# Prompt attention: probabilities scaled in place by GpSimd and turned by plain transposes, in place of fp32 products with diagonals of factors

## The chip, the core and the metric

The kernel runs on one core of a Trainium2 chip. The metric is the device time of one execution in microseconds, the median over repeated runs. The engines are TensorE (PE in the profile), VectorE (DVE), ScalarE (ACT), GpSimd (POOL) and SyncE (SP), each with its own queue, in order, tied together by semaphores.

## What is computed

One inference step of a hybrid decoder layer for 1024 prompt rows and 32 sample rows: half-step FFN, a mixer (attention with three branches and a pooling mixer), a second half-step FFN, and a final norm. The change is in the mixer's attention for the prompt. It has 8 query heads of 64 in two groups, each group with one key/value head. For each head and query row there are three softmaxes: over the compressed keys (64 blocks), over the selected keys (at 16 blocks of 64, all 1024 causal keys), and over a window of 512. Their outputs are added, each with a gate:

```
def masked_softmax(s, mask):
    s = jnp.where(mask, s, NEG_INF)
    m = jnp.max(s, axis=-1, keepdims=True)
    e = jnp.where(mask, jnp.exp(s - m), 0.0)
    return e / jnp.maximum(jnp.sum(e, axis=-1, keepdims=True), 1e-30)

o = gates[..., 0:1] * o_c + gates[..., 1:2] * o_s + gates[..., 2:3] * o_w
```

## The kernel before

The kernel is a row of stages; behind each, all engines meet at a barrier. The order: sample compression, first FFN, input projection, pooling, prompt compression, prompt attention (`stage_attend_prompt`, the only stage that the change touches), sample attention, output projection, second FFN, final norm.

Prompt attention loops over the 2 groups of heads and, in each, over 9 steps. Step `qt` (0 to 7) makes the scores of query tile `qt` (128 query rows) for its four heads, one head at a time: the selected scores over (`qt` + 1) x 128 keys into `slc_bank`, the window and compressed scores into `win_bank`. VectorE finds the maxima (L1744, L1748, L1750). ScalarE writes the exponentials into `probs[qt % 2]` and their sums into `sums` (L1648, L1654, L1656). After the second and the fourth head VectorE works out the factors, gate over sum, for that pair of heads (`factors`, L1704 to L1712).

The same step turns the probabilities of the query tile before, so that keys stand in the partitions, and multiplies them with the values. The work of a tile is cut into units by `value_units`: a unit is one tile of keys of one branch for all four heads. Query tile 0 to 7 has 3, 5, 7, 9, 11, 12, 13 and 14 units, the selected ones first, then the window's, then the compressed one; both groups together have 148. A quarter of a tile's units goes behind each head's scores. The ninth step has no scores, only the 14 units of query tile 7.

A unit goes through four engines' hands. TensorE turns it into one of two banks (`turn`, L1775). ScalarE copies the bank rounded to `turned_hi` (L1624), VectorE writes what was rounded off to `turned_lo` (L1689), and TensorE adds two products with the values into `out_bank` (`value_product`, L1839, L1840). TensorE issues the turn of a unit before the products of the unit ahead of it (`pending`). The banks also serve to turn keys and queries: GpSimd writes each query tile twice over into `dup` (L1582) and TensorE turns it by transposes (L1781). ScalarE's order in a head is: the copy of the first turn, the selected exponential, the copy of the second, the other two exponentials, the rest. VectorE's is: the maxima, then the remainders, then the factors.

The turn of a unit also applies the factors. GpSimd writes, for each pair of heads, six diagonal matrices of the factors (`diagonals`, L1591: the identity times the factors), and `turn` is an fp32 product of the probabilities with such a diagonal, one for each of the four heads. The first unit of a tile waits until both pairs' diagonals are there.

Of the kernel before, what the change touches and what calls it, by code (L numbers as in the profile page):

```python
# [24 lines left out]
ALU = mybir.AluOpType  # L25
AX = mybir.AxisListType

P = 128
# [11 lines left out]
HD, N_HEADS, N_KV, GROUP = 64, 8, 2, 4  # L40
# [1430 lines left out]
def stage_attend_prompt(nc, mem, K, z, kcp, vcp, mixT):  # L1471
# [12 lines left out]
    QT = SEQ // P  # L1484
    WT = WINDOW // P
    NB = SEQ // CMP_STRIDE
    WIN0, CMP0 = SEQ, SEQ + (WT + 1) * P
    PW = CMP0 + NB
    CMP, SLC, WIN = 0, 1, 2
    HEADS = QT * GROUP  # L1490
    PAIR = 2

    def win_tiles(qt):
        return list(range(max(0, qt - WT + 1), qt + 1)) + ([qt - WT] if qt >= WT else [])

    def value_units(qt):
        return ([(SLC, t * P, P, (0, t)) for t in range(qt + 1)]
                + [(WIN, WIN0 + i * P, P, (1, t)) for i, t in enumerate(win_tiles(qt))]
                + [(CMP, CMP0, NB, None)])
# [21 lines left out]
    at = {x: n for n, x in enumerate(order)}  # L1521
    dups = {x: n for n, x in enumerate([x for x in order if x[0] != "v"])}
    products = {x: n for n, x in enumerate([x for x in order if x[0] == "v"])}
    TURNS, DUPS, PRODUCTS = len(order), len(dups), len(products)
    assert TURNS % 2 == 0 and DUPS % 2 == 0 and PRODUCTS % 2 == 0

    ONE, RING = 1, 2
    PE_ORDER, ACT_ORDER, DVE_ORDER = (0, 0), (1, 2), (0, 0)

    with ExitStack() as scope:  # L1530
# [7 lines left out]
        kT_hi = mem.sb(scope, "at_kT_hi", [P, 2, SEQ], F32R)  # L1538
        kT_lo = mem.sb(scope, "at_kT_lo", [P, 2, SEQ], F32R)
        probs = [mem.sb(scope, f"at_probs{i}", [P, GROUP, PW]) for i in range(2)]  # L1540
        diag = mem.sb(scope, "at_diag", [P, 2, GROUP, 3, P])
        neg_max = mem.sb(scope, "at_neg_max", [P, 2, GROUP, 3])
        sums = mem.sb(scope, "at_sums", [P, 2, GROUP, 3])
        factor = mem.sb(scope, "at_factor", [P, 2, GROUP, 3])
# [9 lines left out]
        dup_ready, turned, hi_done, split = (mem.sem("at_dup_ready"), mem.sem("at_turned"),  # L1554
                                             mem.sem("at_hi_done"), mem.sem("at_split"))
# [1 line left out]
        scored = [mem.sem(f"at_scored{i}") for i in range(2)]  # L1557
        maxed = [mem.sem(f"at_maxed{i}") for i in range(2)]
        exped = [mem.sem(f"at_exped{i}") for i in range(2)]
        factor_ready, diag_ready = mem.sem("at_factor_ready"), mem.sem("at_diag_ready")  # L1560
        out_done, upper_done, out_taken = mem.sem("at_out_done"), mem.sem("at_upper_done"), mem.sem("at_out_taken")
        dve_step = mem.sem("at_dve_step")
        STEPS = 2 * 2 * QT + 2
# [1 line left out]
        with nc.Block() as block:  # L1565
            @block.gpsimd
            def _(pool):
                pool.sem_inc(diag_ready, ONE)

                def duplicate(g, x):  # L1570

                    m = dups[x]
                    before = TURNS * g + ONE
                    if m >= 2:
                        before += at[[y for y in dups if dups[y] == m - 2][0]] + 1
                    pool.wait_ge(turned, before)
                    if x[0] == "k":
                        off = (OFF_SLC, OFF_WIN)[x[1]]
                        rows = z[:, 4 * x[2]:4 * x[2] + 4, bass.ds(off + g * HD, HD)]
                    else:  # L1580
                        rows = z[:, x[1], bass.ds(g * GROUP * HD, GROUP * HD)].rearrange("p (r d) -> p r d", r=GROUP)
                    pool.tensor_copy(dup[m % 2][:], rows.unsqueeze(2).to_broadcast([P, 4, 2, HD])).then_inc(dup_ready, 1)  # L1582

                def diagonals(g, qt, pair):
                    pool.wait_ge(factor_ready, 2 * QT * g + 2 * qt + pair + 1)
                    if qt >= 2:
                        last = ("v", qt - 2, len(value_units(qt - 2)) - 1)
                        pool.wait_ge(turned, TURNS * g + at[last] + 1 + ONE)
                    heads = slice(PAIR * pair, PAIR * pair + PAIR)
                    f = factor[:, qt % 2, heads, :]  # L1590
                    pool.tensor_tensor(diag[:, qt % 2, heads].rearrange("p r b n -> p (r b) n"),  # L1591
                                       K["ident"][:].unsqueeze(1).to_broadcast([P, 3 * PAIR, P]),
                                       f.rearrange("p r b -> p (r b)").unsqueeze(2).to_broadcast([P, 3 * PAIR, P]),
                                       ALU.mult).then_inc(diag_ready, 1)

                with pool.Fori(0, N_KV) as g:
                    for x in LEAD:
                        duplicate(g, x)
                    for qt in range(QT):
                        if qt + 1 < QT:  # L1600
                            duplicate(g, ("q", qt + 1))
                        for pair in range(2):
                            diagonals(g, qt, pair)

            @block.scalar
            def _(act):
# [57 lines left out]
            def _(dve):  # L1664
# [28 lines left out]
                def factors(g, qt, pair):  # L1693

                    for i in range(2):
                        dve.wait_ge(exped[i], HEADS * g + GROUP * qt + PAIR * (pair + 1) + ONE)
                    if qt >= 2:
                        dve.wait_ge(diag_ready, 2 * QT * g + 2 * (qt - 2) + pair + 1 + ONE)
                    else:
                        dve.wait_ge(diag_ready, 2 * QT * g + ONE)  # L1700
                    heads = slice(PAIR * pair, PAIR * pair + PAIR)
                    f = factor[:, qt % 2, heads, :]
                    s0 = STEPS * g + (4 * qt + 2 * pair + 2 if qt else 3 * pair)
                    dve.tensor_scalar(f, sums[:, qt % 2, heads, :], 1e-30, None, ALU.max).then_inc(dve_step, 1)  # L1704
                    dve.wait_ge(dve_step, s0 + 1)
                    dve.reciprocal(f, f).then_inc(dve_step, 1)
                    dve.wait_ge(dve_step, s0 + 2)
                    if qt == 0:
                        dve.tensor_scalar(f[:, :, CMP:CMP + 1], f[:, :, CMP:CMP + 1], K["has_block"][:], None,
                                          ALU.mult).then_inc(dve_step, 1)  # L1710
                        dve.wait_ge(dve_step, s0 + 3)
                    dve.tensor_tensor(f, f, z[:, qt, bass.ds(OFF_GATE + g * 3 * GROUP + 3 * PAIR * pair, 3 * PAIR)]  # L1712
                                      .rearrange("p (r b) -> p r b", b=3), ALU.mult).then_inc(factor_ready, 1)
# [12 lines left out]
                with dve.Fori(0, N_KV) as g:  # L1726
# [8 lines left out]
                    for qt in range(QT + 1):  # L1735
                        for r in range(GROUP):
                            if r == 1 and qt >= 2:
                                take(g, qt - 2)
                            n = GROUP * qt + r
# [19 lines left out]
            def _(pe):  # L1759
# [4 lines left out]
                def turn(g, x):  # L1764
                    n = TURNS * g + at[x]
                    bank = turn_bank[at[x] % 2]
                    pe.wait_ge(split, n - 1 + RING)
                    if x[0] == "v":
                        _, qt, u = x
                        branch, lo, rows, _ = value_units(qt)[u]  # L1770
                        if u == 0:
                            pe.wait_ge(diag_ready, 2 * QT * g + 2 * (qt + 1) + ONE)
                        pe.nop(nofuse=True)
                        for h in range(GROUP):
                            tr = pe.matmul(bank[0:rows, h * P:(h + 1) * P], probs[qt % 2][:, h, lo:lo + rows],  # L1775
                                           diag[:, qt % 2, h, branch, :], start=True, stop=True)
                    else:
                        pe.wait_ge(dup_ready, DUPS * g + dups[x] + 1)
                        pe.nop(nofuse=True)
                        for i in range(4):  # L1780
                            tr = pe.transpose(bank[:, i * P:(i + 1) * P],  # L1781
                                              dup[dups[x] % 2][:, i].rearrange("p c d -> p (c d)"), K["ident"][:])
                    tr.then_inc(turned, 1)
# [694 lines left out]
def trunk_step(nc, x_prompt, x_sample, cache_cmp, cache_slc, page_table, state_win, state_pool,  # L2478
# [17 lines left out]
    with ExitStack() as whole:  # L2496
# [21 lines left out]
        with ExitStack() as mixer:  # L2518
            z_sample = mem.sb(mixer, "z_sample", [N_SAMPLE, OFF_POOL])
            with ExitStack() as scope_z:  # L2520
# [22 lines left out]
                with ExitStack() as scope:  # L2543
                    for name, width in (("ident16", P), ("diagonal", P), ("edge", P), ("blocks", 120)):
                        K[name] = mem.sb(scope, name, [P, width], BF16)
                    K["has_block"] = mem.sb(scope, "has_block", [P, 1])
                    with ExitStack() as wide_scope:
                        wide = {name: mem.sb(wide_scope, name + "_wide", [P, width])
                                for name, width in (("diagonal", P), ("edge", P), ("blocks", 120))}
                        stage_constants(nc, mem, [(wide["diagonal"][:], c_diagonal), (wide["edge"][:], c_edge),  # L2550
                                                  (wide["blocks"][:], c_blocks), (K["has_block"][:], c_has_block)],
                                        [(K["ident"][:], K["ident16"][:])]
                                        + [(wide[name][:], K[name][:]) for name in wide])
                    stage_attend_prompt(nc, mem, K, z, kcp[:, 0], vcp[:, 0, 0], trunk)
                    mem.end_stage()
# [87 lines left out]
```

## Time and profile before

| what | value |
|---|---|
| median of 3 runs | 3343.32 us (3338.0 to 3347.6) |
| the profiled execution | 3338.51 us, span 3336.9 us |
| TensorE busy | 2922.3 us, 88% of the span |
| VectorE busy | 1342.8 us, 40% |
| ScalarE busy | 933.8 us, 28% |
| GpSimd busy | 326.9 us, 10% |
| mean granted TensorE clock | 0.929 |

### The profile page before, as it was taken

The numbers are of one execution on the slowest core, as the hardware profiler recorded it, in microseconds if no ns is written. First come the engines' busy times: TensorE is split into PE (matmuls) and PEld (weight loads), VectorE is DVE, ScalarE is ACT, GpSimd is POOL, SyncE is SP. The second block draws the span as 40 slices with busy tenths as digits, with TensorE's granted clock in tenths as the row PEclk, the third lists the DMA queues.
The fourth block names the chain that finished last, engine by engine and source line by source line (L and its number), as shares of the span: only waits on it lengthen the run. The fifth ranks groups of instructions, "written<-read, shape, count | busy, mean of one in ns | idle before, by whom it ended". The sixth has DMA issues, their size and how long they took to land. (4 is left out here: it accounts for less than half of the span.)

```text
span 3336.9 us, 48603 instructions
## 1 busy us (share of the span) xinstructions
PE 2922.3 (88%) x18382; PEld 2686.5 (81%) x18382; DVE 1342.8 (40%) x2566; ACT 933.8 (28%) x1520; POOL 326.9 (10%) x298
## 2 busy tenths in 40 slices
PE   3898878999999997787678789687688999999997
PEld 3898867999999996786567667533587999999996
DVE  6344445433344335113145455322326434344334
ACT  3655633111111112111245445333213111111112
POOL 3444421000000000000011011211001000000000
PEclk9999988999999998898579879888898999999999
DMA  4222132111211102011200000264321111211101
GB/s 155 76 86 108 55 109 91 38 50 38 63 38 38 50 13 86 22 35 42 68 1 1 2 1 1 107 192 152 118 70 38 39 50 38 62 38 38 50 13 52
DMA packets 168573, 193.81 MB, mean 58 GB/s; under 512 B 11432, under 2 KB 154537, under 8 KB 165680
## 3 DMA queue, kind: packets, MB, share of 16 engines
q1 hardware_dynamic: 161623, 141.58, 13.9%
q0 software_dynamic: 6816, 50.49, 4.1%
q8 instruction: 80, 1.31, 0.2%
q14 instruction: 54, 0.43, 0.0%
HBM read 178.30 MB, written 17.91 MB: 59 GB/s over the span
## 5 line engine op out<-in xcount | busy, mean ns | idle before, releaser
L328 ACT ACTIVATE f_act_gate<-f_gate 128x352 f32<-128x352 f32 x132 | 61.2, 465 | 1141.3 <-PE f_gate L104 1141.2
L394 DVE SCALAR_TENSOR_TENSOR trunk<-f_down,trunk 128x352 f32<-128x352 f32 x528 | 276.3, 525 | 209.5 <-PE f_down L104 209.5
L102 PE MATMUL f_gate<-f_h_hi,f_gu_hi 128*128 128x352 f32 x1056 | 343.4, 325 | 15.5 <-DVE f_act_up L370 15.5
L370 DVE TENSOR_TENSOR f_act_up<-f_act_gate,f_up 128x352 f32<-128x352 f32 x132 | 68.8, 521 | 677.7 <-PE f_up L104 632.2
L104 PE MATMUL f_gate<-f_h_hi,f_gu_lo 128*128 128x352 f32 x1056 | 341.0, 323 | 0.0
L103 PE MATMUL f_gate<-f_h_lo,f_gu_hi 128*128 128x352 f32 x1056 | 340.9, 323 | 0.0
L102 PE MATMUL f_up<-f_h_hi,f_gu_hi 128*128 128x352 f32 x1056 | 340.5, 322 | 0.0
L102 PE MATMUL f_down<-f_a_hi,f_wd_hi 128*128 128x352 f32 x1056 | 340.3, 322 | 0.0
L104 PE MATMUL f_down<-f_a_hi,f_wd_lo 128*128 128x352 f32 x1056 | 340.2, 322 | 0.0
L103 PE MATMUL f_down<-f_a_lo,f_wd_hi 128*128 128x352 f32 x1056 | 339.2, 321 | 0.0
L104 PE MATMUL f_up<-f_h_hi,f_gu_lo 128*128 128x352 f32 x1056 | 339.0, 321 | 0.0
L103 PE MATMUL f_up<-f_h_lo,f_gu_hi 128*128 128x352 f32 x1056 | 338.6, 321 | 0.0
L102 PE MATMUL cs_sum<-cs_x_hi,cs_w_hi 128*128 128x256 f32 x768 | 234.8, 306 | 41.2 <-ACT cs_shared L959 22.1
L103 PE MATMUL cs_sum<-cs_x_lo,cs_w_hi 128*128 128x256 f32 x768 | 221.7, 289 | 0.0
L104 PE MATMUL cs_sum<-cs_x_hi,cs_w_lo 128*128 128x256 f32 x768 | 221.2, 288 | 0.0
L102 PEld LDWEIGHTS f_gate<-f_h_hi,f_gu_hi 128*128 128x128 f32 x1056 | 199.9, 189 | 16.3 <-issue 16.0
L103 PEld LDWEIGHTS f_gate<-f_h_lo,f_gu_hi 128*128 128x128 f32 x1056 | 200.2, 190 | 0.2
L104 PEld LDWEIGHTS f_gate<-f_h_hi,f_gu_lo 128*128 128x128 f32 x1056 | 200.3, 190 | 0.0
L104 PEld LDWEIGHTS f_down<-f_a_hi,f_wd_lo 128*128 128x128 f32 x1056 | 199.6, 189 | 0.0
L1775 PEld LDWEIGHTS at_turn_bank<-at_diag,at_probs 128*128 128x128 f32 (+1 forms) x1184 | 162.9, 204 | 45.5 <-issue 39.6
L1775 PE MATMUL at_turn_bank<-at_diag,at_probs 128*128 128x128 f32 (+1 forms) x1184 | 178.0, 298 | 24.5 <-POOL at_diag L1591 20.3
L104 PEld LDWEIGHTS f_up<-f_h_hi,f_gu_lo 128*128 128x128 f32 x1056 | 198.7, 188 | 0.0
(331 smaller groups left out, 5892.6 us busy)
## 6 DMA issues: line engine op xcount, KB each, us to landing
as_pages<-in_cache_kv_slc_dram SPq DMA_DIRECT2D x192, 128.0 KB, 2.3
f_gu_raw<-in_w_ffn_gate_dram SPq DMA_DIRECT2D x44, 512.0 KB, 4.3
f_gu_raw<-in_w_ffn_up_dram SPq DMA_DIRECT2D x44, 512.0 KB, 5.6
f_wd_raw<-in_w_ffn_down_dram SPq DMA_DIRECT2D x22, 1024.0 KB, 5.0
as_pages<-in_cache_kv_slc_dram POOLq DMA_DIRECT2D x64, 128.0 KB, 3.3
in_w_raw<-in_w_in_dram SPq DMA_DIRECT2D x4, 1304.0 KB, 5.9
x_saved<-trunk SPq DMA_DIRECT2D x1, 4224.0 KB, 16.7
trunk<-x_saved SPq DMA_DIRECT2D x1, 4224.0 KB
```

What stands on the lines that cost most here:

```text
L102: pe.matmul(out, w_hi, x_hi, start=first, stop=False)
L103: pe.matmul(out, w_hi, x_lo, start=False, stop=False)
L104: return pe.matmul(out, w_lo, x_hi, start=False, stop=last)
L328: act.activation(act_gate[:, b, :], gate_bank[b][:, 0:CH], ACT.Silu).then_inc(silu_done, 1)
L370: dve.tensor_tensor(act_up[:], act_gate[:, b, :], up_bank[b][:, 0:CH], ALU.mult).then_inc(pair_free, 1)
L394: dve.scalar_tensor_tensor(xT[:, m, chunk(c)], down_bank[n % 4][:, 0:CH], 0.5, xT[:, m, chunk(c)], ALU.mult, ALU.add).then_inc(down_free, 1)
L1775: tr = pe.matmul(bank[0:rows, h * P:(h + 1) * P], probs[qt % 2][:, h, lo:lo + rows], diag[:, qt % 2, h, branch, :], start=True, stop=True)
```

## The change

GpSimd no longer writes diagonals. `scale` multiplies the probabilities in place by the factor of their row, one instruction for each head and branch: for a pair of heads first the two selected parts, then the two window parts, then the two compressed ones. The semaphore `scaled` is raised after the selected and after the compressed parts, twice a pair. `turn` is a plain transpose against the identity, four for a unit. Selected units wait for the selected parts of both pairs, window and compressed ones for all parts. The wait of `diagonals` for the turns of two tiles before, which guarded the ring of diagonals, is gone with the tile `diag`. VectorE's wait before it writes factors is on `scaled` with the counts that fit. The probabilities still have two buffers, and everything else stands as it was.

```diff
--- before.py
+++ after.py
@@ -1538,7 +1538,6 @@
         kT_hi = mem.sb(scope, "at_kT_hi", [P, 2, SEQ], F32R)
         kT_lo = mem.sb(scope, "at_kT_lo", [P, 2, SEQ], F32R)
         probs = [mem.sb(scope, f"at_probs{i}", [P, GROUP, PW]) for i in range(2)]
-        diag = mem.sb(scope, "at_diag", [P, 2, GROUP, 3, P])
         neg_max = mem.sb(scope, "at_neg_max", [P, 2, GROUP, 3])
         sums = mem.sb(scope, "at_sums", [P, 2, GROUP, 3])
         factor = mem.sb(scope, "at_factor", [P, 2, GROUP, 3])
@@ -1557,7 +1556,7 @@
         scored = [mem.sem(f"at_scored{i}") for i in range(2)]
         maxed = [mem.sem(f"at_maxed{i}") for i in range(2)]
         exped = [mem.sem(f"at_exped{i}") for i in range(2)]
-        factor_ready, diag_ready = mem.sem("at_factor_ready"), mem.sem("at_diag_ready")
+        factor_ready, scaled = mem.sem("at_factor_ready"), mem.sem("at_scaled")
         out_done, upper_done, out_taken = mem.sem("at_out_done"), mem.sem("at_upper_done"), mem.sem("at_out_taken")
         dve_step = mem.sem("at_dve_step")
         STEPS = 2 * 2 * QT + 2
@@ -1565,7 +1564,7 @@
         with nc.Block() as block:
             @block.gpsimd
             def _(pool):
-                pool.sem_inc(diag_ready, ONE)
+                pool.sem_inc(scaled, ONE)
 
                 def duplicate(g, x):
 
@@ -1581,17 +1580,17 @@
                         rows = z[:, x[1], bass.ds(g * GROUP * HD, GROUP * HD)].rearrange("p (r d) -> p r d", r=GROUP)
                     pool.tensor_copy(dup[m % 2][:], rows.unsqueeze(2).to_broadcast([P, 4, 2, HD])).then_inc(dup_ready, 1)
 
-                def diagonals(g, qt, pair):
+                def scale(g, qt, pair):
+
                     pool.wait_ge(factor_ready, 2 * QT * g + 2 * qt + pair + 1)
-                    if qt >= 2:
-                        last = ("v", qt - 2, len(value_units(qt - 2)) - 1)
-                        pool.wait_ge(turned, TURNS * g + at[last] + 1 + ONE)
-                    heads = slice(PAIR * pair, PAIR * pair + PAIR)
-                    f = factor[:, qt % 2, heads, :]
-                    pool.tensor_tensor(diag[:, qt % 2, heads].rearrange("p r b n -> p (r b) n"),
-                                       K["ident"][:].unsqueeze(1).to_broadcast([P, 3 * PAIR, P]),
-                                       f.rearrange("p r b -> p (r b)").unsqueeze(2).to_broadcast([P, 3 * PAIR, P]),
-                                       ALU.mult).then_inc(diag_ready, 1)
+                    pool.nop(nofuse=True)
+                    w = len(win_tiles(qt)) * P
+                    for branch, lo, n in ((SLC, 0, (qt + 1) * P), (WIN, WIN0, w), (CMP, CMP0, NB)):
+                        for r in range(PAIR * pair, PAIR * pair + PAIR):
+                            p = probs[qt % 2][:, r, lo:lo + n]
+                            last = pool.tensor_scalar(p, p, factor[:, qt % 2, r, branch:branch + 1], None, ALU.mult)
+                        if branch != WIN:
+                            last.then_inc(scaled, 1)
 
                 with pool.Fori(0, N_KV) as g:
                     for x in LEAD:
@@ -1600,7 +1599,7 @@
                         if qt + 1 < QT:
                             duplicate(g, ("q", qt + 1))
                         for pair in range(2):
-                            diagonals(g, qt, pair)
+                            scale(g, qt, pair)
 
             @block.scalar
             def _(act):
@@ -1695,9 +1694,9 @@
                     for i in range(2):
                         dve.wait_ge(exped[i], HEADS * g + GROUP * qt + PAIR * (pair + 1) + ONE)
                     if qt >= 2:
-                        dve.wait_ge(diag_ready, 2 * QT * g + 2 * (qt - 2) + pair + 1 + ONE)
+                        dve.wait_ge(scaled, 2 * (2 * QT * g + 2 * (qt - 2) + pair + 1) + ONE)
                     else:
-                        dve.wait_ge(diag_ready, 2 * QT * g + ONE)
+                        dve.wait_ge(scaled, 4 * QT * g + ONE)
                     heads = slice(PAIR * pair, PAIR * pair + PAIR)
                     f = factor[:, qt % 2, heads, :]
                     s0 = STEPS * g + (4 * qt + 2 * pair + 2 if qt else 3 * pair)
@@ -1768,12 +1767,14 @@
                     if x[0] == "v":
                         _, qt, u = x
                         branch, lo, rows, _ = value_units(qt)[u]
-                        if u == 0:
-                            pe.wait_ge(diag_ready, 2 * QT * g + 2 * (qt + 1) + ONE)
+                        if branch != WIN:
+                            pe.wait_ge(scaled, 4 * QT * g + 4 * qt + (3 if branch == SLC else 4) + ONE)
+                        else:
+                            pe.wait_ge(scaled, 4 * QT * g + 4 * qt + 4 + ONE)
                         pe.nop(nofuse=True)
                         for h in range(GROUP):
-                            tr = pe.matmul(bank[0:rows, h * P:(h + 1) * P], probs[qt % 2][:, h, lo:lo + rows],
-                                           diag[:, qt % 2, h, branch, :], start=True, stop=True)
+                            tr = pe.transpose(bank[0:rows, h * P:(h + 1) * P], probs[qt % 2][:, h, lo:lo + rows],
+                                              K["ident"][:])
                     else:
                         pe.wait_ge(dup_ready, DUPS * g + dups[x] + 1)
                         pe.nop(nofuse=True)
```

## Rows read from the trace of the kernel before

**Rows 1.** The profile's page, part 1: busy us, share of span, instructions.
```profile
PE 2922.3 (88%) x18382; PEld 2686.5 (81%) x18382; DVE 1342.8 (40%) x2566; ACT 933.8 (28%) x1520; POOL 326.9 (10%) x298
```

**Rows 2.** Windows of prompt attention: busy us and count by engine, granted clock (PEclk), DMA share.
```profile
1668.00:2137.00 469.00, 394.96 (x2312) 318.88 (x2312) 247.03 (x531) 219.22 (x578) 59.69 (x54) 0.87 0.00 1
1668.00:1700.00 32.00, 22.87 (x101) 19.64 (x102) 13.63 (x40) 12.59 (x47) 5.95 (x7) 0.50 0.00 1
1749.00:1843.00 94.00, 83.95 (x536) 67.89 (x534) 55.59 (x111) 47.89 (x119) 12.42 (x11) 0.96 0.00 1
```

**Rows 3.** Waits, 1660 to 2140: who waited for whom, us in total, times, longest.
```profile
ACT at_turned_hi L1624 <- PE at_turn_bank L1775: 191.7, 102, 4.8
...
PE at_turn_bank L1775 <- POOL at_diag L1591: 20.3, 14, 3.1
```

**Rows 4.** Groups by line and shape, 1660 to 2140: count, busy us, mean ns, idle before.
```profile
L1775 PE MATMUL at_turn_bank<-at_diag,at_probs 128*128 128x128 f32 x1056 | 160.6, 301 | 24.5 <-POOL at_diag L1591 20.3 <-PE at_out_bank L1840 2.1 <-DVE at_turned_lo L1689 1.0
...
L1591 POOL TENSOR_TENSOR at_diag<-ident,at_factor 128x768 f32<-128x768 f32 x32 | 47.0, 1468 | 343.8 <-DVE at_factor L1712 343.8
...
L1781 PE MATMUL at_turn_bank<-ident,at_dup 128*128 128x128 f32 x96 | 21.1, 372 | 15.9 <-DVE at_kc_lo L1674 8.3 <-issue 4.6 <-DVE at_kT_lo L1681 3.0
...
L1582 POOL COPY at_dup<-z 128x512 f32 x24 | 14.5, 611 | 359.7 <-PEq L1760 321.1 <-PE at_turn_bank L1775 25.8 <-PE at_turn_bank L1781 12.7
```

**Rows 5.** Groups by line, GpSimd, whole span.
```profile
L895 POOL TENSOR_TENSOR cs_x_lo<-cs_x,cs_x_hi 128x512 fp32r<-128x512 f32 x128 | 165.9, 1296 | 259.4 <-ACT cs_x_hi L952 259.4
```

**Rows 6.** Timeline of TensorE, 2030 to 2044: start, us, what, [idle before it].
```profile
2031.40 0.64 PE L1781 MATMUL at_turn_bank<-ident,at_dup 128*128 128x128 f32 x4
2031.87 1.06 PE L1775 MATMUL at_turn_bank<-at_diag,at_probs 128*128 128x128 f32 x8
...
2037.00 0.39 PE L1786 MATMUL at_slc_bank<-at_kT_hi,at_q_split 128*128 128x512 f32 x1
...
2038.90 1.14 PE L1775 MATMUL at_turn_bank<-at_diag,at_probs 128*128 128x128 f32 x8
2039.80 0.48 PE L1839 MATMUL at_out_bank<-at_turned_hi,at_v_split 128*128 128x512 f32 x1
...
2041.62 0.48 PE L1839 MATMUL at_out_bank<-at_turned_hi,at_v_split 128*128 128x512 f32 x1 [0.22 <-DVE at_turned_lo L1689]
...
2043.84 0.39 PE L1786 MATMUL at_slc_bank<-at_kT_hi,at_q_split 128*128 128x512 f32 x1
```

**Rows 7.** Timeline of ScalarE in the same head.
```profile
2040.65 0.89 ACT L1648 ACTIVATE at_probs<-at_slc_bank,at_neg_max 128x768 f32<-128x768 f32 x1
...
2042.01 0.80 ACT L1654 ACTIVATE at_probs<-at_win_bank,at_neg_max 128x640 f32<-128x640 f32 x1
...
2042.97 0.22 ACT L1656 ACTIVATION_READ_ACCUMULATOR at_probs<-at_win_bank,at_neg_max 128x1 f32 x1
```

**Rows 8.** Timeline of TensorE, last step of a group, no scores.
```profile
1888.82 1.05 PE L1775 MATMUL at_turn_bank<-at_diag,at_probs 128*128 128x128 f32 x8
...
1891.45 0.48 PE L1839 MATMUL at_out_bank<-at_turned_hi,at_v_split 128*128 128x512 f32 x1 [0.23 <-DVE at_turned_lo L1689]
...
1892.00 1.05 PE L1775 MATMUL at_turn_bank<-at_diag,at_probs 128*128 128x128 f32 x8
```

**Rows 9.** Timeline of TensorE at half clock, 1683 to 1697.
```profile
1683.84 1.09 PE L1781 MATMUL at_turn_bank<-ident,at_dup 128*128 128x128 f32 x4
...
1693.50 2.06 PE L1775 MATMUL at_turn_bank<-at_diag,at_probs 128*128 128x128 f32 x8
1696.87 0.55 PE L1786 MATMUL at_slc_bank<-at_kT_hi,at_q_split 128*128 128x256 f32 x1 [1.31 <-ACT at_probs L1648]
```

**Rows 10.** Timeline of TensorE at the last step's edge.
```profile
2109.56 0.84 PE L1775 MATMUL at_turn_bank<-at_diag,at_probs 128*128 128x128 f32 x4 [3.06 <-POOL at_diag L1591]
```

**Rows 11.** Windows of sample attention: all instructions, then tile as_kt_bank's alone.
```profile
2197.00:2217.00 20.00, 17.08 (x128) 7.15 (x128) 4.20 (x11) 8.11 (x17) 4.30 (x8) 1.00 0.56 175
...
2197.00:2217.00 20.00, 5.13 (x32) 3.45 (x32) 0.00 (x0) 5.31 (x9) 1.00 0.56 175
```

## The prediction

> **What bounds the kernel now.** I read the page first: TensorE is busy for 88% of the span, no other engine for over 40% [rows 1]. So whatever TensorE is relieved of can shorten the run, if nothing else in the changed stage then holds it. The change touches one stage, prompt attention, 469 us long (1668 to 2137); nothing of it overlaps another stage, because each ends in a barrier of all engines. The windows of it [rows 2] show TensorE busy 395 of 469 us at a granted clock of 0.87, in the first 32 us only 0.50. That share is nearly as high as in the rest, but a busy TensorE here is mostly latency of short matmuls. So I looked at the waits of the stage [rows 3]: ScalarE waits 192 us for turns of TensorE, and TensorE is held by GpSimd's diagonals for 20 us. So TensorE sets the pace, with ScalarE and VectorE close behind it in each round.
>
> The timeline shows how. A unit (one tile of 128 keys of four heads) goes through a ring of two banks: four turns on TensorE, a rounded copy on ScalarE, the remainder on VectorE, then two products with the values on TensorE. In the stretch without scores at the end of each group [rows 8] a turn starts at 1888.82, takes 1.05, its product starts at 1891.45 (1.58 us after the turn ended), and the turn after the next starts 0.55 behind that, at 1892.00. With two units in flight that is a loop: (1.05 + 1.58 + 0.55) / 2 = 1.59 us for one unit. TensorE's own work on a unit is 0.80 to 0.90 for the turn and 0.55 for the products, so loop and engine are about equal bounds.
>
> **TensorE's part.** Removed are 592 fp32 products (148 units of four, 1184 records of 298 ns on average); added are 592 transposes. Each product is two records, each transpose one [rows 4]. At full clock four transposes take 0.64 from the first start to the last end and hold TensorE for 0.47 (2031.40 to 2031.87); eight records of products take 1.05 to 1.14 and hold it for 0.82 to 0.90 [rows 6]. So a turn ends 0.42 to 0.5 earlier, and TensorE is free 0.4 earlier. At half clock it is 2.06 against 1.09 [rows 9]. If all of it came through, that would be 148 x 0.4 = 59 us, more with the cold units. It won't, for three kinds of stretch:
>
> 1. The last step of each group, 14 units without scores, 28 in all: the loop becomes (0.63 + 1.58 + 0.55) / 2 = 1.38, a gain of 0.21 a unit, 5.9 us.
>
> 2. Steps 4 to 7, where the units of query tiles 3 to 6 are turned, 9 + 11 + 12 + 13 = 45 a group, 90 in all. Take the head from 2037.00 to 2043.84, 6.84 us with three units [rows 6]. Scores take 1.90. Then the first turn ends at 2.53 instead of 3.04, and its product can start at about 4.2 instead of 4.62. The second and third copy now meet ScalarE's exponentials: the selected part holds it for 0.89 and the reading of its sum, window and compressed part from 2042.01 to 2043.19 [rows 7], so the second copy starts only at 4.0 and the second product at 5.5. The head ends at 6.0, a gain of 0.8 for three units. The same walk with four units gives 0.65. That is 0.16 to 0.27 a unit; at 0.22 x 90 it is 20 us.
>
> 3. Steps 1 to 3, 3 + 5 + 7 units a group. There TensorE waits for ScalarE before the next scores (1.31 us at 1696.87 [rows 9]), because ScalarE's first work of a head is the copy of the turn. The chain turn, copy, exponential, scores is shortened by the whole latency once a head: 22 heads by 0.42 warm or 0.97 cold, at 0.65 about 14 us, and about 1 us for the second units of a head.
>
> Sum: 5.9 + 20 + 15 = 41 us.
>
> **GpSimd's part.** Removed are 32 multiplications of 128x768, 1.47 each [rows 4]. Added are 192 scalings, 71,680 elements a partition (36 tiles selected, 30 tiles window, 8 x 64 compressed, by eight heads). The trace of before has no such instruction. The nearest row is the copy with one input, 611 ns for 512 elements, 1.19 ns each with its fixed part [rows 4]. The diagonals give 1.91, and the slowest elementwise row of this engine, a subtraction with two inputs and a rounded output, 1296 / 512 = 2.53 [rows 5]. I take 1.19, since one tensor is read and one written; 1.91 and 2.53 are kept for the range. At 1.19 GpSimd works 85 us instead of 47 of the 469, and in step 7 the scaling of a pair of heads (3,456 elements, 4.1 us) ends before the other pair's factors are there, a head of some 6 us later.
>
> What counts is the wait at each step's edge: the first turn of a query tile needs the second pair's factors, which VectorE writes last. Now it waits for one diagonal of 1.47; the longest such wait is 3.06 at 2109.56 [rows 10]. Then it will wait for two scalings of (qt + 1) x 128 elements; the window part is not needed until all selected units are turned. Over query tiles 1 to 7 that is 256 x 35 x 1.19 = 10.7 us in place of 7 x 1.47 = 10.3 a group: 1 us more in both groups. At 1.91 it is 14 us more, at 2.53 it is 25 us more. Query tile 0 has no unit in the first quarter. Scores are now done a little earlier against the factors, 0.15 a step: 2 us. Behind the wait stand the next head's scores, so all of it is on the path. Together 3 us. The duplicates of q, queued behind the scalings, are needed only in the third head of a step, two heads later. VectorE's instructions with tensors in SBUF alone are the factors, four short ones a pair; I cost a clash at nothing, at most one scaling each.
>
> The Trainium skill (GPSIMD Engine Reference, section 3.1) has 1.03 cycles per element for bodies with up to two operations at 1.2 GHz, 0.86 ns; by that estimate the edges would be 5 us shorter than now, not 1 longer. No run here shows it yet.
>
> **The clock.** TensorE is granted 0.50 in the first 32 us, where it waits a lot, and 0.96 in 1749 to 1843 [rows 2]. The change takes half of the array's work out of every turn while the latencies stay. I expect the clock to fall at more step edges, where TensorE waits 1 to 3 us, and to rise later in steps 1 to 3. My estimate is 45 us more at half clock (0.87 down to 0.82). The price: a head of three units is 6.0 us warm; cold, scores double to 3.8 and a unit costs 0.86 + 1.0, together 9.4, so a cold microsecond does a third less. 45 x 0.3 = 14 us. Both ends: nothing if the clock holds, 25 us if it is lost for 80 us.
>
> **The sum.** 41 - 3 - 14 = 24 us less. The profiled execution took 3338.5 (span 3336.9), so it would be 3314.5. The median of the runs is 3343.3, 4.8 above it, so on the scale of the median 3319 us.
>
> **Rivals.** (a) Faster still: the clock holds, and with the 3 us gone too (or the skill's price of a scaling) the gain is 38 to 50 us, 3293 to 3305. For it: in steps 5 to 7 TensorE stays dense. Against it: the edges already cost clock now.
> (b) No change: the edges at 1.91 ns per element (14 us) and the clock at its worst end (25 us) eat the 41; 3335 to 3350.
> (c) Slower by GpSimd: at 2.53 ns the pair of step 7 takes 8.7 us, longer than a head, so the second pair's scalings start late as well; I get 2 us in step 7 and about 1.5 in each of steps 4 to 6, some 10 us in all, beside the 25 at the edges and 25 of clock: 19 us slower, 3362. It turns slower from about 2.2 ns per element with the clock at its worst end, and needs 2.9 with the clock as I expect. For it: only the slowest row; that has two inputs.
> (d) Slower by clock: transposes don't count as work for the clock, so that the whole stage runs at half. From cold durations: 148 units x 1.86 = 275, scores 140, other turns and waits 90, together 505 in place of 469: 3380. Against it: in the sample attention, 2197 to 2217, the clock was 1.00 although 32 of the 128 matmuls, 5.1 of 17.1 us, were transposes into the key bank [rows 11].
> The Trainium skill (TensorE: Matmul & The Clock Gate, Part 4) states this rule: transpose mode doesn't count as a busy TensorE in the same way and the full clock doesn't engage. The rows speak against its strong form.
>
> **Chances.** Forecast (gain 12 to 36, 3307 to 3331) 0.53; (a) 0.18; (b) 0.16; (c) 0.08; (d) 0.05. A measurement of this kernel tells about 0.3% (10 us) from no change. Faster 0.72, within 0.15, slower 0.13. The range for 8 in 10 takes in (a) and (b): 3290 to 3348; the likeliest case's own is 3307 to 3331.
>
> **What would show it.** Right: the turns' line has 592 records in place of 1184 with four of them in 0.63 us; a pitch of about 1.4 us in the last step; scalings of about 1.2 ns per element; TensorE's wait for GpSimd near 23 us in the stage; granted clock of the stage 0.80 to 0.84; nothing outside the stage moved. The forecast falls if a scaling costs 2 ns per element, if the copies on ScalarE queue deeper than I walked through, or if the clock of the stage drops under 0.75.

## Result and profile after

The changed kernel takes 3375.45 us (median of 4 runs, 3374.7 to 3376.6) against 3342.17 us: ratio 1.010, 95% interval 1.0087 to 1.0113. It is 33 us slower where 24 us faster was forecast; rival (c), slower by GpSimd, had the direction and the cause, at a chance of 0.08 and a time of 3362.

The profiled execution has a span of 3373.0 us. The page's part 1, then the window of the stage (busy us and count by engine, granted clock), the waits of TensorE in it, and the groups by line and shape:

```profile
PE 2868.8 (85%) x17790; PEld 2619.2 (78%) x17790; DVE 1348.7 (40%) x2566; ACT 931.6 (28%) x1520; POOL 509.6 (15%) x458
```
```profile
1669.00:2171.00 502.00, 340.85 (x1719) 251.89 (x1719) 252.73 (x531) 216.95 (x578) 242.05 (x214) 0.79 0.00 1
```
```profile
PE at_turn_bank L1776 <- issue: 81.7, 14, 9.4
...
PE at_out_bank L1840 <- DVE at_turned_lo L1688: 40.6, 60, 1.9
```
```profile
L1776 PE MATMUL at_turn_bank<-ident,at_probs 128*128 128x128 f32 x528 | 99.3, 321 | 89.5 <-issue 81.7 <-DVE at_q_split L1683 4.8 <-DVE at_turned_lo L1688 3.0
...
L1591 POOL TENSOR_SCALAR at_probs<-at_probs,at_factor 128x640 f32<-128x640 f32 x40 | 74.9, 1888 | 28.2 <-DVE at_factor L1711 28.2
...
L1591 POOL TENSOR_SCALAR at_probs<-at_probs,at_factor 128x64 f32<-128x64 f32 x64 | 27.5, 447 | 0.0
...
L1591 POOL TENSOR_SCALAR at_probs<-at_probs,at_factor 128x1024 f32<-128x1024 f32 x8 | 22.7, 2849 | 32.0 <-DVE at_factor L1711 32.0
```

The stage grew from 469 us [rows 2] to 502, which is the whole loss. TensorE does less in it (341 us busy, 395 before) and waits more: 81.7 us in 14 waits ahead of the first turn of a tile, where it was 20.3 us in 14 [rows 3]. (Expectations below say 84 and 23: they count the 3 us of waits for a free bank as well.) The granted clock of the stage is 0.79 in place of 0.87. A scaling takes (2849 - 447) / (1024 - 64) = 2.50 ns per element and 0.29 us fixed. GpSimd is busy for 242 us of the stage; it had been 60.

The wait reads "issue", which means that the profile names no releaser. The timeline of an edge shows it. This is the edge ahead of the last step in the first group of heads: GpSimd, VectorE and TensorE, with the start, the length in us, what ran, and the idle time before it:

```profile
1880.07 20.41 POOL L1591 TENSOR_SCALAR at_probs<-at_probs,at_factor 128x1024 f32<-128x1024 f32 x12 [15.97 <-DVE at_factor L1711]
```
```profile
1887.36 0.17 DVE L1711 TENSOR_TENSOR at_factor<-at_factor,z 128x6 f32<-128x6 f32 x1
```
```profile
1896.03 1.08 PE L1776 MATMUL at_turn_bank<-ident,at_probs 128*128 128x128 f32 x4 [9.41 <-issue]
```

The second pair's factors were there at 1887.5. GpSimd was still on the first pair until 1880.07 + 2 x (2.85 + 1.89 + 0.45) = 1890.4, and two selected parts of 2.85 bring it to 1896.1; TensorE starts at 1896.03. So the 9.4 us of waiting are 0.9 until the second pair's factors were there, 2.9 of the first pair's backlog and 5.7 of the second pair's own selected parts, within 0.1. The same wait of the other group was 3.06 in the kernel before [rows 10].

What the forecast had right also shows. In the step without scores [rows 8] two turns now come in 2.72 us, so one each 2.72 / 2 = 1.36 us (forecast 1.38; 1.59 before):

```profile
1906.31 0.60 PE L1776 MATMUL at_turn_bank<-ident,at_probs 128*128 128x128 f32 x4
...
1909.03 0.60 PE L1776 MATMUL at_turn_bank<-ident,at_probs 128*128 128x128 f32 x4
```

### The profile page after: what moved, and what is told of

It reads as the page before. It is cut to its first block and busy times, and to the rows that moved or that the text cites. A ratio compares the mean times of both kernels' runs of the same rounds, so it can differ in the third digit from the quotient of the medians.

```text
span 3373.0 us, 47575 instructions
## 1 busy us (share of the span) xinstructions
PE 2868.8 (85%) x17790; PEld 2619.2 (78%) x17790; DVE 1348.7 (40%) x2566; ACT 931.6 (28%) x1520; POOL 509.6 (15%) x458
## 5 line engine op out<-in xcount | busy, mean ns | idle before, releaser
L1591 POOL TENSOR_SCALAR at_probs<-at_probs,at_factor 128x64 f32<-128x64 f32 (+8 forms) x192 | 229.4, 1220 | 213.4 <-DVE at_factor L1711 213.2
L895 POOL TENSOR_TENSOR cs_x_lo<-cs_x,cs_x_hi 128x512 fp32r<-128x512 f32 x128 | 166.1, 1298 | 259.8 <-ACT cs_x_hi L952 259.8
```

Source lines behind the costliest of these rows:

```text
L895: pool.tensor_tensor(x_lo[s][:, 0:ODD], x[s][:, 0:ODD], x_hi[s][:, 0:ODD].bitcast(F32), ALU.subtract).then_inc(diff_lo_done, 1)
L1591: last = pool.tensor_scalar(p, p, factor[:, qt % 2, r, branch:branch + 1], None, ALU.mult)
```

## Experiments

The theory was that the loss is GpSimd's scalings, waited for at the edges of the steps; its rivals were that the transposes cost the clock what they save, and that the second pair's own selected parts alone count. All ratios are against the kernel before on the same chip, whose median there was 3339.9 to 3342.1 us.

**Nothing scaled.** GpSimd only raises the semaphore; the output for the prompt is then that of unscaled probabilities.

```diff
-                    for branch, lo, n in ((SLC, 0, (qt + 1) * P), (WIN, WIN0, w), (CMP, CMP0, NB)):
...
+                    pool.sem_inc(scaled, 2)
```

> GpSimd multiplies nothing and only raises the semaphore when the factors are there, so the probabilities stay unscaled; the transposes and all other work are as in the changed kernel. Theory 1 (the loss is GpSimd's scalings at 2.5 ns per element, waited for at the edges of the steps, 84 us of waits in place of 23): the waits at the edges all but vanish, the transposes' own gain stays, 3275 to 3300 us, granted clock of the stage 0.84 or more. Theory 2 (transposes don't keep the clock up, and the stage loses by that): still 3330 or more, clock of the stage under 0.80.

3268.7 us, ratio 0.978 (0.9764 to 0.9797): theory 1, by more than expected. The same head as in [rows 6], the fourth of step 5 in the second group, runs from 1985.00 to 1991.03, 6.03 us against 6.84 (forecast 6.0), two rows of TensorE's timeline:

```profile
1985.00 0.39 PE L1782 MATMUL at_slc_bank<-at_kT_hi,at_q_split 128*128 128x512 f32 x1
...
1991.03 0.39 PE L1782 MATMUL at_slc_bank<-at_kT_hi,at_q_split 128*128 128x512 f32 x1
```

**Products with the identity.** The changed kernel with the old kind of turn.

```diff
-                            tr = pe.transpose(bank[0:rows, h * P:(h + 1) * P], probs[qt % 2][:, h, lo:lo + rows],
-                                              K["ident"][:])
+                            tr = pe.matmul(bank[0:rows, h * P:(h + 1) * P], probs[qt % 2][:, h, lo:lo + rows],
+                                           K["ident"][:], start=True, stop=True)
```

> The changed kernel, but each turn is an fp32 product with the identity in place of a transpose; GpSimd's scalings stay. Theory 1: the transposes save TensorE time outside the edges, some 30 us or more, so this is 3400 to 3420 us, with the same waits of 84 us at the edges. Theory 2: transposes gave back by the clock what they saved, so this is 3365 to 3385 us with a higher granted clock.

3419.5 us, ratio 1.0235 (1.0218 to 1.0252): theory 1. Its waits, and the window of its stage:

```profile
PE at_turn_bank L1776 <- issue: 73.4, 14, 8.8
```
```profile
1669.00:2215.00 546.00, 421.66 (x2309) 341.57 (x2310) 251.77 (x534) 219.34 (x579) 242.59 (x216) 0.80 0.00 1
```

This splits the change in two. Against the kernel before only the scaling differs: 79 us slower. Against the changed kernel only the kind of turn differs: transposes are worth 3419.5 - 3375.5 = 44 us (41 forecast; beside the first of the two the kernel before took 3340.5 us, beside the second 3342.2). 79 - 44 = 35, measured 33. Of the 79, 73.4 - 20.3 = 53 are waits; that the other 26 are clock is worked out, not isolated: a clock of 0.80 over 546 us is 218 us at half clock, 0.87 over 469 is 122. And the clock is 0.80 with products and 0.79 with transposes, so the transposes are not what lowers it. (The 44 us are net: with transposes the waits are 8 us longer, 81.7 against 73.4.)

**Selected parts first.** GpSimd's order within a query tile: selected parts of pair one, of pair two, then the rest.

```diff
-                        for pair in range(2):
-                            scale(g, qt, pair)
+                        for pair in range(2):
+                            scale(g, qt, pair, [(SLC, 0, (qt + 1) * P)])
+                        for pair in range(2):
+                            scale(g, qt, pair, [(WIN, WIN0, w), (CMP, CMP0, NB)])
```

> The changed kernel, but GpSimd scales the selected parts of both pairs of a query tile before the window and compressed parts of either. Theory 1a (half of a wait at an edge is the first pair's scalings still in GpSimd's queue): the 84 us of waits fall to about 45 (two selected parts at 2.5 ns per element), time 3330 to 3345 us. Theory 1b (only the second pair's own selected parts count): unchanged within 5 us, 3370 to 3380.

3340.9 us, ratio 1.0001 (0.9991 to 1.001): theory 1a. The waits:

```profile
PE at_turn_bank L1777 <- issue: 51.0, 14, 6.8
```

31 of the 82 us were the first pair's window and compressed parts, queued ahead of the second pair's selected ones. Order alone takes back the whole loss.

**All scalings on VectorE**, behind the factors of each pair:

```diff
+                    dve.wait_ge(factor_ready, 2 * QT * g + 2 * qt + pair + 1)
...
+                            last = dve.tensor_scalar(p, p, factor[:, qt % 2, r, branch:branch + 1], None, ALU.mult)
```

> VectorE does all 192 scalings right behind the factors, GpSimd none. If VectorE takes 0.5 to 1.1 ns per element, 37 to 75 us more on an engine that is busy 253 of 502 us: the wait at the last edge falls from 9.4 to 1 to 2.5 us and the time to 3300 to 3325 us, faster than both kernels. Rival: its maxima of the next heads come late behind the scalings, ScalarE and TensorE wait for them, 3340 or more.

3327.7 us, ratio 0.9951 (0.9934 to 0.9967), between the two cases. VectorE takes 750 ns for 1024 elements, 0.52 ns each beyond a fixed 0.2 us, and TensorE's waits at the edges fall to 7.1 us in all, the longest 2.5. But VectorE's other work comes late: ScalarE waits 35.4 us for maxima, where it was 10.3 before, and TensorE 70.2 us for remainders, where it was 40.6 in the changed kernel:

```profile
L1717 DVE TENSOR_SCALAR at_probs<-at_probs,at_factor 128x1024 f32<-128x1024 f32 x8 | 5.7, 750 | 0.1
```
```profile
PE at_out_bank L1847 <- DVE at_turned_lo L1687: 70.2, 61, 3.3
ACT at_probs L1646 <- DVE at_neg_max L1750: 35.4, 32, 2.7
```

**TensorE kept busy at the edges.** Products whose result is overwritten, ahead of the wait:

```diff
+                        if u == 0:
+                            pe.nop(nofuse=True)
+                            for _ in range((0, 10, 14, 21, 23, 25, 29, 37)[qt]):
+                                pe.matmul(bank[:, 0:P], K["ident"][:], K["ident"][:], start=True, stop=True)
```

> The changed kernel, with 10 to 37 more fp32 products of the identity with itself (their result is overwritten) issued by TensorE at each edge of a step, ahead of its wait for GpSimd, sized to 0.8 of the wait at about 0.2 us each. The waits for the scalings stay as long. Theory A (the waits also cost clock, and the clock costs time): granted clock of the stage rises from 0.79 to 0.85 or more and the time falls by 8 to 20 us, to 3355 to 3367. Theory B (the waits alone are the price, the lower clock is hidden behind ScalarE and VectorE): 3372 to 3378.

3351.5 us, ratio 1.0034 (1.0022 to 1.0046): theory A, with 24 us back where 8 to 20 were expected. GpSimd is as busy as in the changed kernel (242 us); the products fill the waits but for 10.2 us, which the profile now puts down to GpSimd by name, and the granted clock of the stage moved from 0.79 to 0.92:

```profile
PE at_turn_bank L1780 <- POOL at_probs L1591: 10.2, 14, 1.2
```

```profile
1669.00:2149.00 480.00, 378.99 (x2356) 298.48 (x2356) 251.87 (x531) 217.37 (x579) 241.83 (x214) 0.92 0.00 1
```

**The same in the kernel before**, with (0, 5, 5, 4, 4, 4, 3, 12) products for query tiles 0 to 7.

> The kernel before, with 3 to 12 more fp32 products of the identity at each edge, ahead of the wait for GpSimd's diagonals (23 us of waits). It asks how much of a wait's price is clock where the waits are short. The changed kernel got back 24 us from 84 us of waits this way, 0.28 a microsecond. By that share: 3333 to 3337 against 3340. Rival: waits of 1 us hardly cost clock, and the products in the way cost as much as they bring, 3338 to 3343.

3323.2 us, ratio 0.9945 (0.9932 to 0.9959), 19 us less where about 5 were expected. So keeping TensorE busy wins nearly as much over its short waits (0.9 to 3.1 us) as over the long ones (2.7 to 9.4 us). The stage's clock rises from 0.87 to 0.92:

```profile
1669.00:2122.00 453.00, 389.74 (x2453) 316.16 (x2452) 247.55 (x534) 219.31 (x578) 59.19 (x53) 0.92 0.01 2
```

**Two inputs on GpSimd.** The factor spread over the row, both heads at once:

```diff
+                        f = factor[:, qt % 2, heads, branch]
+                        last = pool.tensor_tensor(p, p, f.unsqueeze(2).to_broadcast([P, PAIR, n]), ALU.mult)
```

> The changed kernel, but GpSimd scales with 96 products of two inputs (the factor spread over the row, both heads of a pair in one instruction) in place of 192 scalings by a scalar. Theory A (the price is the scalar form's): about 1.9 ns per element as the diagonals took, waits at the edges 84 down to about 60 us, 3345 to 3358 us. Theory B (this engine takes about 2.5 ns per element for anything that reads a tensor and multiplies): 3370 to 3380.

3320.4 us, ratio 0.9942 (0.9927 to 0.9958), 55 us under the changed kernel, more than theory A gave (3345 to 3358). GpSimd's groups and TensorE's wait:

```profile
L1592 POOL TENSOR_TENSOR at_probs<-at_probs,at_factor 128x2048 f32<-128x2048 f32 x4 | 14.4, 3603 | 38.3 <-DVE at_factor L1712 38.3
L1592 POOL TENSOR_TENSOR at_probs<-at_probs,at_factor 128x128 f32<-128x128 f32 x32 | 12.8, 401 | 0.0
```
```profile
PE at_turn_bank L1777 <- issue: 31.4, 14, 4.8
```

(3603 - 401) / 1920 = 1.67 ns per element and 0.19 us fixed, in half as many instructions. The diagonals had the very same price: 768 x 1.67 + 190 = 1.47 us [rows 4].

**VectorE for the second pair's selected parts**, GpSimd (scalar form, selected first) for the rest:

```diff
+                    if pair in (1,):
+                        dve.wait_ge(factor_ready, 2 * QT * g + 2 * qt + pair + 1)
+                        for r in range(PAIR * pair, PAIR * pair + PAIR):
+                            p = probs[qt % 2][:, r, 0:(qt + 1) * P]
+                            last = dve.tensor_scalar(p, p, factor[:, qt % 2, r, SLC:SLC + 1], None, ALU.mult)
+                        last.then_inc(scaled_too, 1)
```

> The selected parts of the second pair, the ones an edge waits for, are scaled by VectorE right behind the factors at 0.52 ns per element, and the rest by GpSimd with selected parts first. VectorE gets some 17 us more work, not 69. Expected: waits at the edges about 25 us, 3295 to 3315 us, faster than all versions so far. Rival: VectorE and GpSimd get in each other's way when both scale, VectorE's scalings take 1 us or more in place of 0.55 and the time stays at 3320 or more.

3308.6 us, ratio 0.9904 (0.9889 to 0.992), within what was expected. VectorE's scalings took 0.98 us in place of 0.75 at 1024 elements, which the rival had named, but it did not cost the gain.

**VectorE for the selected parts of both pairs.**

> VectorE scales the selected parts of both pairs, GpSimd the window and compressed parts. VectorE gets some 35 us more work. If VectorE's load is what kept the version with all scalings on it at 3328, this lands between it and the version with the second pair's alone, 3305 to 3320 us. If GpSimd's first pair is late in that other version, this one is the faster of the two.

3308.8 us, ratio 0.9906 (0.9891 to 0.9921): no difference from the last. The waits of TensorE show two changes that cancel. Waits for scalings at the edges fall by 9 us, waits for remainders grow by 13. First the version with the second pair alone, then this one:

```profile
PE at_out_bank L1848 <- DVE at_turned_lo L1689: 42.0, 64, 1.7
PE at_turn_bank L1784 <- DVE at_probs L1718: 23.4, 13, 3.1
```
```profile
PE at_out_bank L1845 <- DVE at_turned_lo L1687: 55.2, 54, 2.6
...
PE at_turn_bank L1781 <- DVE at_probs L1716: 14.7, 12, 3.2
```

**Both engines, two inputs on GpSimd.**

> VectorE scales the selected parts of the second pair, GpSimd the rest with products of two inputs (1.67 ns per element and 0.19 us each, against 2.50 and 0.29 for the scalar form). If GpSimd was still late in the version that scaled the rest in the scalar form (3309 us), this one gains: 3295 to 3306 us. Rival: GpSimd had slack there, and the edge is set by VectorE's own two scalings; 3306 to 3311.

3327.3 us, ratio 0.9956 (0.9943 to 0.997): a miss for both expectations, 19 us slower than with the scalar form, though GpSimd is faster. VectorE's scaling of 1024 elements, first beside the scalar form, then beside two inputs:

```profile
L1718 DVE TENSOR_SCALAR at_probs<-at_probs,at_factor 128x1024 f32<-128x1024 f32 x4 | 3.7, 979 | 0.1
```
```profile
L1719 DVE TENSOR_SCALAR at_probs<-at_probs,at_factor 128x1024 f32<-128x1024 f32 x4 | 7.0, 1781 | 0.1
```

With GpSimd idle it took 750. The mean of 1781 hides two kinds: of the two scalings at an edge, the first takes 0.75 us and the second 2.81. VectorE and GpSimd at the edge ahead of the first group's last step:

```profile
1874.20 0.75 DVE L1719 TENSOR_SCALAR at_probs<-at_probs,at_factor 128x1024 f32<-128x1024 f32 x1
...
1874.87 2.81 DVE L1719 TENSOR_SCALAR at_probs<-at_probs,at_factor 128x1024 f32<-128x1024 f32 x1
```
```profile
1874.31 2.82 POOL L1591 TENSOR_TENSOR at_probs<-at_probs,at_factor 128x1280 f32<-128x1280 f32 x1 [1.37 <-DVE at_factor L1713]
```

GpSimd's instruction needs 2.32 us when VectorE does not scale; here it takes 0.5 more, and VectorE's second scaling ends only 0.55 us behind it. That is what taking turns by whole instructions would look like. At the same edge beside the scalar form the second scaling takes 1.21 us. So the form that is faster for GpSimd made the edge slower, since the edge waits for just these scalings: TensorE's waits for VectorE's scalings and GpSimd's are 32.5 + 6.1 us in place of 23.4 + 0.8. That is 14 of the 19 us; the rest, with a stage clock of 0.81 in place of 0.84, was not taken apart.

```profile
PE at_turn_bank L1785 <- DVE at_probs L1719: 32.5, 12, 4.7
...
PE at_turn_bank L1785 <- POOL at_probs L1591: 6.1, 2, 3.2
```

**The same, kept busy at the edges**, (0, 3, 4, 8, 7, 8, 6, 12) products.

> As the version with both engines, with 3 to 12 fp32 products of the identity at each edge, ahead of its wait. If the 27 us of waits there cost clock at the same rate, 5 to 10 us less than that version and the granted clock of the stage up from 0.84 to 0.88 or more. Rival: within 2 us of it.

3315.4 us, ratio 0.9921 (0.9907 to 0.9934), 12 us back where 5 to 10 were expected, clock of the stage 0.81 to 0.90.

**The best split, kept busy.**

> The best version so far (3309 us: VectorE scales the second pair's selected parts, GpSimd the rest in the scalar form), with 3 to 12 fp32 products of the identity at each edge, ahead of its wait. The same products took 12 us off the version with two inputs on GpSimd. If that is the price of the clock: 3294 to 3302, granted clock of the stage up from 0.84 to 0.90 or more. Rival: with waits of 1 to 3 us little is left to win, 3304 to 3310.

3294.8 us, ratio 0.9861 (0.9843 to 0.9878), as expected: 14 us under the same split without the products, 46 us under the kernel before, the fastest version here that computes everything. Its stage:

```profile
1669.00:2095.00 426.00, 323.85 (x1912) 245.62 (x1912) 273.68 (x566) 218.10 (x579) 192.28 (x182) 0.91 0.01 2
```

## Why the prediction was wrong

**The price of a scaling failed**, and with it the term of 3 us for GpSimd. "I take 1.19, since one tensor is read and one written": it was 2.50 ns per element and 0.29 us fixed, and TensorE's waits at the edges grew by 81.7 - 20.3 = 61 us. The path was right (the first turn of a tile waits for the second pair's selected parts), and so was the sign named for a fall, a scaling of 2 ns per element or more. The copy was the nearest row by the number of its inputs, and the wrong one; an upper bound of 2.53, taken from another kind of instruction, happened to hold. At the measured price the forecast's own formula gives the waits that were seen behind the right order: 2.50 x 256 x 35 + 14 x 0.29 us = 26.5 a group in place of 10.3, 32 us more in both, against 51.0 - 20.3 = 31. With the two-input form (1.67) the change is a gain: 3320 us. That this meets the forecast's 3319 is luck, since its terms are others.

**The queue at the edge was undersized.** I let the first pair's scalings end before the second pair's factors came; at 2.5 ns they end 2.9 us after them in the last step. The walk had 4.1 us for a pair in step 7, well inside a head; it took 10.4. Rival (c) allowed 10 us for this (its own items, in both groups, sum to 13), and the order of the selected parts showed 31. It put the second pair's own parts at 25 us where 31 were measured, the fixed 0.29 left out, and the clock at 25, where 26 were worked out. That is why (c) said 3362 and not 3375.

**TensorE's part held in its sum, and partly by luck in its places.** 41 us were forecast, 44 measured with the long waits in place. The timelines with products and with transposes, split by head (from its first product of selected scores to the next head's), give 13 us in steps 1 to 3 (forecast 15), 22 in steps 4 to 7 (forecast 20) and 10 in the last steps (forecast 6), less 1 us for a longer wait at the last edges. But of the 22, 14 lie in the eight heads behind an edge, where TensorE is at half clock and a turn saves 0.97 us in place of 0.42 [rows 9, 6]; the other 24 heads gave 7 together. The walk through the fourth head was right, 6.03 us for 6.0. It was carried over to heads where it does not hold: the third heads of steps 5 and 6, in which a query tile is turned as well, took 7.50 to 7.75 us in the kernel before and in the version with nothing scaled.

The turn itself is shorter than taken: at full clock four transposes hold TensorE for 0.35 us, not 0.47. The loop of the last step was a good bound (1.38 forecast, 1.36 seen). Products waited longer for VectorE's remainders, as the walk had it: 40.6 us in the changed kernel (its line stands above), against this line of the kernel before:

```profile
PE at_out_bank L1839 <- DVE at_turned_lo L1689: 13.4, 39, 0.9
```

**The clock** was put at 0.82 for waits of 23 us; with waits of 82 us it was 0.79, 211 us at half clock in place of 122. The price of a microsecond at half clock, 0.3, fits the 26 us for 96 that were worked out above (0.27). The runs kept busy give 24 us for 134 less at half clock in the changed kernel (0.18) and 19 for 50 in the kernel before (0.38), so it is a figure of 0.2 to 0.4 at best. What I missed is that the clock had a price in the kernel before: 19 us could be had there without the change. Rival (d), transposes that don't count for the clock, fell: 0.80 with products and 0.79 with transposes at waits of 73 and 82 us. The strong form of the rule in the Trainium skill (TensorE: Matmul & The Clock Gate, Part 4) is not borne out here: in the last step of the first group, where 40 of the 59 matmuls are transposes and the rest products of the values, the granted clock was 0.99. A stretch of transposes alone was not run.

```profile
1902.00:1915.00 13.00, 10.08 (x59) 7.46 (x58) 7.44 (x14) 6.04 (x11) 0.00 (x0) 0.99 0.00 1
```

**The clash of VectorE and GpSimd**, put at nothing, exists in the changed kernel too, but it is small. The remainders take 691 ns as before. The first instruction of the factors, which works in SBUF alone, took up to 709 ns beside the scalings; before, and in the changed kernel (shortest, median, longest in ns):

```profile
L1704 DVE TENSOR_SCALAR at_factor<-at_sums x32: 151/161/173, 1686.3 to 2107.2; 128x6 f32<-128x6 f32 x32
```
```profile
L1703 DVE TENSOR_SCALAR at_factor<-at_sums x32: 150/164/709, 1687.2 to 2139.4; 128x6 f32<-128x6 f32 x32
```

That is about 4 us in the stage. GpSimd was still busy with the first pair at the slow ones, so no run shows a price. The clash mattered once VectorE scaled too.

## What to carry to other kernels

Price a GpSimd instruction by a row with the same operation and form, or keep the slowest row as the forecast and not as the edge of the range: a factor of two in it turned 24 us of gain into 33 of loss. When work is moved to a slow engine, split it by when each part is needed and queue the needed parts first; the order alone was worth 35 us. In these runs a wait of TensorE cost its length and then some clock, so look at short regular waits for a gain even where nothing else changes. And look behind a mean: one of 1781 ns was made of 753 and 2811.

## What the runs showed of the hardware

- GpSimd, fp32 in place: by a scalar of the partition 2.50 ns per element and 0.29 us, by a second input spread over the row 1.67 ns and 0.19 us. The Trainium skill (GPSIMD Engine Reference, section 4.1) calls one-input work roughly line rate and two-input work about twice as slow as on VectorE. The copy is near it (1.19 ns with its fixed part in it). The scalar form is not, and is the slower of the two. No run here has the two-input product on VectorE, so the factor of two is not shown.
- VectorE's scaling of 128x1024 took 750 ns with GpSimd idle. Beside GpSimd's scalar form it took 0.75 us (the first of two) and 1.21 (the second), beside its two-input form 0.75 and 2.81, ending only when GpSimd's instruction of 2.82 us was over. GpSimd's 128x1280 went from 2322 to 2502 on average. VectorE's remainders, which read one input from PSUM, stayed at 691. The Trainium skill (GPSIMD Engine Reference, section 1) names SBUF interfaces that the two engines share; the rows agree with that.
- A stage of 469 us had 14 waits of TensorE of 0.9 to 3.1 us each, 20 us in all. Filling them with products that nobody reads raised the granted clock of the stage from 0.87 to 0.92 and made a kernel that was otherwise unchanged 19 us faster.
